# Linear attention in half steps between the units of the column projection, its values projected in token layout

## The reference, cut to what matters

```python
h = rmsnorm(x, norm_g)
proj = h @ w_in                       # split into g_q g_k g_v g_lr g_gate, f_*, m_*
log_a = log_sigmoid(g_lr @ w_alpha_up + b_alpha) / 16.0
# GLA: 4 heads, key width 48, value width 96, chunks of C = 64
b = cumsum(log_a, within a chunk)
q_dec = q * K ** -0.5 * exp(b); k_dec = k * exp(-b); k_to_end = k * exp(b_last - b)
attn = (q_dec @ k_dec.T) * causal
S_next = exp(b_last) * S + k_to_end.T @ v
o = attn @ v + q_dec @ S
o_gla = rmsnorm(o, gla_norm_g) * silu(g_gate)
# forgetting attention (6 heads, "fox") and attention over 256 memory tokens (4 heads, "att")
out = x + concat(o_gla, o_fox, o_mem) @ w_out   # then a final rmsnorm
```

## Time and profile before

| | before |
|---|---|
| runs, median | 1478.14 us |
| profiled execution, span | 1480.9 us |
| TensorE busy | 1312.8 us (89%) |
| VectorE, ScalarE, POOL busy | 665.6, 576.9, 411.6 us |
| mean granted clock of TensorE | 0.942 |
| column projection, matmuls L644 | x2112, 481.6 us busy |

### The profile page before, as it was taken

One profiled execution on the slowest core, in us unless ns is written; L12 is line 12 of the kernel. 1 busy time (PEld: TensorE's weight loads), 2 busy tenths in 40 slices (PEclk: granted clock), 3 DMA queues, 4 the chain that ended last, 5 costly groups with the idle time before them and its releaser, 6 DMA issues. The chain is left out here.

```text
span 1480.9 us, 20787 instructions
## 1 busy us (share of the span) xinstructions
PE 1312.8 (89%) x6576; PEld 1053.3 (71%) x6576; DVE 665.6 (45%) x1606; ACT 576.9 (39%) x1154; POOL 411.6 (28%) x408
## 2 busy tenths in 40 slices
PE   5898989999999999938785985999899999599997
PEld 4887878888888888814453663777678687478886
DVE  4563311110000011178874763888788798432222
ACT  3563201111111000047652874777677777421010
POOL 5223420111111011044553577222322422300000
PEclk9999999999999999959876987999999999799999
DMA  5453333331222121165321543422623520355553
GB/s 201 144 164 118 111 111 113 127 120 64 70 78 78 64 78 58 49 177 166 109 85 60 165 113 84 115 93 61 156 63 94 122 59 12 98 207 198 199 174 137
DMA packets 98908, 166.45 MB, mean 112 GB/s; under 512 B 10740, under 2 KB 51444, under 8 KB 96996
## 3 DMA queue, kind: packets, MB, share of 16 engines
q1 hardware_dynamic: 96088, 156.97, 34.7%
q10 hardware_dynamic: 2560, 8.39, 1.4%
q0 software_dynamic: 192, 0.33, 0.1%
HBM read 101.36 MB, written 64.29 MB: 112 GB/s over the span
## 5 line engine op out<-in xcount | busy, mean ns | idle before, releaser
L644 PE MATMUL col_cps<-h_T,tok_slot 128*128 128x512 f32 x2112 | 481.6, 390 | 4.0 <-POOL tok_slot L600 3.9
L644 PEld LDWEIGHTS col_cps<-h_T,tok_slot 128*128 128x128 f32 x2112 | 397.9, 188 | 87.8 <-issue 4.9
L1736 PE MATMUL out_yps<-out_w,out_mix 128*128 128x512 f32 x768 | 177.7, 394 | 19.3 <-DMA out_mix<-scr_mix 16.8
L1736 PEld LDWEIGHTS out_yps<-out_w,out_mix 128*128 128x128 f32 x768 | 145.7, 190 | 51.1 <-DMA out_mix<-scr_mix 17.1
L1540 ACT ACTIVATE fox_pT<-fox_tps 128x512 fp32r<-128x512 f32 x240 | 124.8, 531 | 88.2 <-PE fox_tps L1473 85.5
L1578 DVE TENSOR_SCALAR_CACHE_REDUCE fox_prob<-fox_sps 128x512 f32<-128x512 f32 (+2 forms) x240 | 142.0, 606 | 36.6 <-PE fox_sps L1463 33.7
L1589 DVE TENSOR_TENSOR fox_pT<-fox_tps,fox_pT 128x512 fp32r<-128x512 f32 x240 | 141.6, 604 | 21.7 <-ACT fox_pT L1540 20.9
L1473 PE MATMUL fox_tps<-all_ident,fox_prob 128*128 128x128 f32 x816 | 134.6, 278 | 15.1 <-ACT fox_prob L1532 8.2
L707 DVE COPY tok_xn<-col_cps 128x512 f32<-128x512 f32 x24 | 16.6, 692 | 287.4 <-PE col_cps L644 287.4
L1486 PE MATMUL fox_ops<-fox_pT,fox_v 128*128 128x512 f32 x480 | 137.2, 376 | 0.0
L1473 PEld LDWEIGHTS fox_tps<-all_ident,fox_prob 128*128 128x128 f32 x816 | 99.9, 141 | 45.1 <-ACT fox_prob L1532 11.6
(11 more groups left out here) (189 smaller groups left out, 1760.3 us busy)
## 6 DMA issues: line engine op xcount, KB each, us to landing
scr_split<-tok_w SPq DMA_DIRECT2D x64, 256.0 KB, 2.7
out_mix<-scr_mix SPq DMA_DIRECT2D x32, 512.0 KB, 4.2
tok_xin<-in_w_cols SPq DMA_DIRECT2D x22, 512.0 KB, 3.8
tok_xin<-in_x SPq DMA_DIRECT2D x16, 512.0 KB, 3.7
scr_gates<-tok_xn SPq DMA_DIRECT2D x32, 256.0 KB, 2.3
out_x<-in_x SPq DMA_DIRECT2D x16, 512.0 KB, 6.2
out<-out_o ACTq DMA_DIRECT2D x16, 512.0 KB, 4.9
scr_fox_v<-tok_vst SPq DMA_DIRECT2D x16, 384.0 KB, 2.9
```

The source lines that it names most:

```text
L644: mm = nc.tensor.matmul(cps[c][:, :], w[s][a_][:, kk, :], hT[b_][:, kk, c * CH:(c + 1) * CH], start=(kk == 0 and n == 0), stop=(kk == KT - ...
L1736: mm = nc.tensor.matmul(yps[s][:, c, :], mix[s][a][:, kk, :], w[b][:, kk, c * CH:(c + 1) * CH], start=(kk == 0 and n == 0), stop=(kk == MI ...
```

## The change

`project_columns` and `gated_linear_attention` become one stage, `columns_and_linear_attention`, written out over the 88 units instead of in loops. The tiles come in another order: 3 of GLA values, 3 of GLA queries and keys ("raw"), 3 of GLA gates, 8 split ones, 5 gates. TensorE has two banks for the units instead of four, since the linear attention takes the other six.

- A unit of the values is made in token layout: the normalised tokens are the stationary operand and the 128 weight columns move. That is 96 matmuls 128 wide in place of 24 that are 512 wide. The values' transposes (L920) and the copies of them on ScalarE are gone, and so is `vz`: the chunk states are made from 64 rows each, two for each pair of heads.
- Decay logits, Abs, Exp, Ln and the scan for 512 tokens lie ahead of units 6, 8, 10 and 12. Their `b` goes to scratch memory.
- Step n of the linear attention lies ahead of units 36 + 2n and 37 + 2n, one half at each. Inputs are loaded for one step (128 tokens) at a time; the Exps and the decayed queries and keys for step n + 1 are made in the second half of step n.
- The fills and first loads of the memory head and the fox head move to the start of the memory attention, on VectorE and SP ahead of all else.
- The tiles that the token stage leaves free lie elsewhere in SBUF, so that they can be released.

The diff's core:

```diff
+    KINDS = ["value"] * 3 + ["raw"] * 3 + ["gate"] * 3 + ["split"] * NSPLIT + ["gate"] * (NGATE - 3)
+    G0 = 36
+    def step_at(cls, u):
+        n, half = divmod(u - cls.G0, 2)
+        return (n, half) if -2 <= n <= cls.STEPS else (None, half)
...
+    Z_UNITS = {6 + 2 * g: g for g in range(NCH)}
...
+            @block.sync
...
+                for u in range(CU.UNITS):
+                    j, c = divmod(u, NCH)
+                    if c == 0 and j + 2 < NCOL:
+                        sp.wait_ge(w_lo, j + 1)
+                        sp.dma_start(w_raw[j % 2][:, :, :], w_cols[j + 2]).then_inc(cols_loaded[j % 2], 16)
+                    if u in Z_UNITS:
+                        g = Z_UNITS[u]
+                        if g == 0:
+                            sp.wait_ge(rows_stored, 80)
+                        if g >= 2:
+                            sp.wait_ge(z_done, PAIRS * (g - 1))
+                        sp.dma_start(lr[g % 2][:, :], scr.lr[:, g * CH:(g + 1) * CH]).then_inc(lr_loaded[g % 2], 16)
...
+                        if half_step == 0:
+                            if n + 2 < NS:
+                                load_inputs(n + 2)
+                            if 0 <= n < NS:
+                                load_gate(n)
+                        else:
+                            if 0 <= n + 1 < NS:
+                                load_values(n + 1)
+                            if n >= 1:
+                                store_mix(n - 1)
+                    store_unit(u)
...
+                def store_unit(u):
...
+                    sp.wait_ge(evacuated, u + 1)
...
+            @block.tensor
...
+                def decay_logits(g):
+                    pe.wait_ge(lr_loaded[g % 2], 16 * (g // 2 + 1))
...
+                for u in range(CU.UNITS):
+                    j, c = divmod(u, NCH)
+                    if u in Z_UNITS:
+                        decay_logits(Z_UNITS[u])
+                    n, half_step = CU.step_at(u)
+                    if n is not None:
+                        if half_step == 0:
+                            if n >= 1:
+                                outputs(n - 1)
+                            if 0 <= n < NS:
+                                key_side(n)
+                        else:
+                            if 0 <= n < NS:
+                                chunk_states(n)
+                            if n >= 1:
+                                transposed_outputs(n - 1)
+                    if c == 0:
+                        pe.wait_ge(w_lo, j + 1)
+                    if u >= 2:
+                        pe.wait_ge(evacuated, u - 1)
+                    if CU.KINDS[j] == "value":
+                        for i in range(CH // P):
+                            tokens = slice((4 * c + i) * P, (4 * c + i + 1) * P)
+                            for kk in range(KT):
+                                for r, (a_, b_) in enumerate(PASSES):
+                                    mm = nc.tensor.matmul(cps[u % 2][:, i * P:(i + 1) * P], hT[a_][:, kk, tokens],
+                                                          w[j % 2][b_][:, kk, :],
+                                                          start=(kk == 0 and r == 0), stop=(kk == KT - 1 and r == 2))
...
+                def key_side(n):
+                    if n:
+                        pe.wait_ge(k_copied, n)
+                    pe.wait_ge(prep_done, n + 1)
...
+                def chunk_states(n):
...
+                        for e in range(2):
+                            rows = slice(GLA_C * e, GLA_C * (e + 1))
+                            mm = nc.tensor.matmul(kvps[e][0:KR, p * W2:(p + 1) * W2], kt[rows, p * KR:(p + 1) * KR],
+                                                  vt[n % 2][rows, p * W2:(p + 1) * W2], start=True, stop=True)
...
+            @block.vector
...
+                        if half_step == 0:
+                            if 0 <= n < NS:
+                                mask(n)
+                            if n >= 1:
+                                normalise(n - 1)
+                            if 0 <= n + 1 < NS:
+                                decay_to_end(n + 1)
+                        else:
+                            if 0 <= n < NS:
+                                advance_states(n)
+                            if n >= 1:
+                                gated(n - 1)
+                            if 0 <= n + 1 < NS:
+                                decayed_queries(n + 1)
+                    evacuate(u)
...
+            @block.gpsimd
...
+                    if c == 0 and j >= 1 and j + 1 < NCOL:
+                        split(j + 1)
...
+                        if half_step == 0:
+                            if n >= 1:
+                                rstds(n - 1)
+                            if 0 <= n < NS:
+                                gates(n)
+                        else:
+                            if n >= 1:
+                                split_mix(n - 1)
+                            if 0 <= n + 1 < NS:
+                                decayed_keys(n + 1)
...
-def softmax_attention(nc, scr, ident, ident_b, mask, first, next_stages):
+def softmax_attention(nc, scr, ident, ident_b, mask, first, opening, next_stages):
...
+                for head in opening:
+                    head.first_loads(sp)
                 load_gate(0, 0)
                 load_gate(0, 1)
...
+                for head in opening:
+                    head.first_fill(nc.vector)
                 round_(0, False, prologue=True)
...
-            gated_linear_attention(nc, scr, ident, gla_mask, w_alpha_up, b_alpha, gla_norm_g, (att_head, fox_head))
-            softmax_attention(nc, scr, ident, ident_b, fox_mask, att_head, (weights_out,))
-        softmax_attention(nc, scr, ident, ident_b, fox_mask, fox_head, ())
+            softmax_attention(nc, scr, ident, ident_b, fox_mask, att_head, (att_head, fox_head), (weights_out,))
+        softmax_attention(nc, scr, ident, ident_b, fox_mask, fox_head, (), ())
```

More of the change, by code:

```diff
@@ L712, in gated_linear_attention, with gate_index, sends, sent_before @@
-def gated_linear_attention(nc, scr, ident, gla_mask, w_alpha_up, b_alpha, gla_norm_g, next_stages):
-    NG, GT = T // CH, CH
-    NS = T // P
-    ST = CH // P
+class ColumnUnits:
+    KINDS = ["value"] * 3 + ["raw"] * 3 + ["gate"] * 3 + ["split"] * NSPLIT + ["gate"] * (NGATE - 3)
+    FIRST = {"value": 0, "raw": 3, "split": 9}
+    UNITS = NCOL * NCH
+    G0 = 36
+    STEPS = T // P
+    @classmethod
+    def gate_index(cls, j):
+        return j - 6 if j < 9 else j - 9 - NSPLIT + 3
+    @classmethod
+    def sends(cls, u):
+        return 2 if cls.KINDS[u // NCH] == "split" else 1
+    @classmethod
+    def sent_before(cls, u):
+        return 16 * sum(cls.sends(i) for i in range(u % 2, u, 2))
+    @classmethod
+    def step_at(cls, u):
+        n, half = divmod(u - cls.G0, 2)
+        return (n, half) if -2 <= n <= cls.STEPS else (None, half)
@@ L743, in gated_linear_attention @@
         gn = k.sb("gn", [P, 3])
+        bf = k.sb("bf", [FOX_H, 1])
+        dec = [k.sb(f"dec{s}", [KR, PAIRS, P // GLA_C]) for s in range(2)]
+        ss, ms, rstd, half = (k.sb(n, [P, GLA_H]) for n in ("ss", "ms", "rstd", "half"))
+        cps = [k.ps(f"cps{s}", [P, CH]) for s in range(2)]
+        rows_ctx = ExitStack()
+        with rows_ctx:
+            kr = Pools(nc, rows_ctx, "rows")
+            rT, a_full = kr.sb("rT", [FGLR, T]), kr.sb("a", [FOX_H, T])
+            parts = [kr.sb(f"part{i}", [FOX_H, T], F32R) for i in (HI, LO)]
+            rps = kr.ps("rps", [P, T])
@@ new lines, in columns_and_linear_attention @@
+        f, a = rT[0:FOX_H, :], a_full[:, :]
+        decay_ctx = ExitStack()
+        with decay_ctx:
+            kz = Pools(nc, decay_ctx, "decay")
+            lr = [kz.sb(f"lr{s}", [GLA_R, CH]) for s in range(2)]
+            keep, zabs, la, bz = (kz.sb(n, [KR, PAIRS, CH]) for n in ("keep", "zabs", "la", "b"))
+        q, kk_, b = ([k.sb(f"{n}{s}", [KR, PAIRS, P]) for s in range(2)] for n in ("q", "k", "b"))
+        tail, ep, em, ee, kd, kte = (k.sb(n, [KR, PAIRS, P]) for n in "tail ep em ee kd kte".split())
@@ L772, in gated_linear_attention @@
[L772 to L785 removed]
+        kps, aps, ops, ots = (k.ps(n, [P, CH]) for n in ("kps", "aps", "ops", "ots"))
@@ new lines, in load_values, with load_gate @@
+                def load_values(n):
+                    if n >= 2:
+                        sp.wait_ge(o_done, n - 1)
+                    sp.dma_start(vt[n % 2][:, :], scr.gla_v[n]).then_inc(v_loaded[n % 2], 16)
+                def load_gate(n):
+                    if n >= 2:
+                        sp.wait_ge(mixed, n - 1)
+                    else:
+                        for parity in range(2):
+                            sp.wait_ge(stored[parity], CU.sent_before(4 * 9 + parity))
+                    sp.dma_start(gate[n % 2][:, :, :], scr.gates[0:3, :, n * P:(n + 1) * P].rearrange("j p t -> p j t")
```

(5 more changed lines are left out.)

990 lines of the change are left out of this document (408 added, 582 removed).

## The result

The changed kernel takes 1550.5 us, the kernel before 1478.1; the ratio is **1.0483, 95% interval 1.0461 to 1.0505**: slower by 4.8%. Forecast was 1486 (+8), the range ended at 1522. The direction was right, the size was not: some 60 us are missing from the sum, most of them because the narrow value matmuls ran at half the clock for much of their time.

The account below looks back on a forecast made before the run. TensorE fills the column projection; a chain through four engines bounds the linear attention. -179.7 + 16.6 + 70.7 + 76.3 + 8.8 + 16 + 4.4 - 5.0 = +8.1 on 1480.9, less 2.8: forecast 1486 us, range 1459 to 1522.

Parts of the forecast that it names:

- The value term, +70.7: Value units on TensorE: 1152 narrow matmuls at 0.118 us, 135.9 us, replace 65.2 us of wide ones; bounds +30 to +74.
- The rival of the falling clock: Value units: narrow matmuls leave the array half empty and the clock falls, up to +136 us, 1622; chance 0.03.
- The dips, +4.4: Clock dips after the four waits before the decay logits, 1.1 us lost in each.
- Decay logits, +8.8: Decay logits on TensorE between column units: eight matmuls, each two records of 1.11 us together.
- Waits for the rows, +16: TensorE waits for the low-rank rows `lr` before each of four decay-logit groups, 4.0 us each.
- Steps, +76.3: Linear attention's TensorE work between column units: 16 steps of 4.77 us, nothing taken for overlap or breaks.
- Opening of the memory attention, +16.6: Start of memory attention: loads ahead of the gates on SP delay POOL's first gate to 30.5 us from 13.9.
- the term's upper bound: Memory attention's opening: +24 us if the second head's loads are late too, by their own issue of 7.4.
- POOL's chain in the second half: Linear attention step, second half: 7.9 us chain against 9.1 before TensorE asks, margin 1.2, so costed at nothing.
- the third rival: POOL's chain late in the second half of each step: 2 us beyond the margin give 1518; chance 0.14.
- The standstill of 3.88 us: Column projection: TensorE's wait for the third tile's weight split on POOL disappears with its clock dip, -5.0 us.
- The stage removed, -179.7: The 183.3 us between column projection and memory attention go, except a stage change that remains.

Follow-up runs that it names:

- gates_first: Changed kernel with SP issuing both gates and the second head ahead of the fox head's first loads: 1545.3 and 1548.6 us, and 1606.3 and 1607.2.
- before_narrow: Kernel before with only its last three column tiles, the value tiles, as 1152 matmuls of 128 columns: 1542.8 us, ratio 1.042.
- spread_loads: Changed kernel with wide, transposed values, earlier low-rank rows and reordered loads (1445.6 us), now with the fox head's loads spread in pieces, output weights later: 1436.5 us.
- after_again: Changed kernel, unchanged, profiled a second time: 1604.9 and 1613.0 us.
- lr_early_warm: Changed kernel with low-rank rows loaded one unit earlier and 48 wide matmuls ahead of the first value unit: 1537.6 us, ratio 1.038.
- warm_again: lr_early_warm with 24 more wide matmuls in front of each of units 6, 8 and 10: 1495.7 us, ratio 1.010.
- halves_256: Changed kernel with value units as 576 matmuls of 256 columns, weights stationary, output not the reference's: 1449.8 us, ratio 0.980.

## Why the prediction was wrong

For the kernel after in its shorter executions the span is 1546.9 to 1548.8 where my sum had 1489.0: 58 to 60 us to account for. (The timed runs are 63 above the forecast, since the profiled execution of the kernel before was some 4 us longer than its median run.) Point by point, with `gates_first` for the value units:

- **The value term, +70.7, is the step that failed.** It measured 188.9 - 65.2 = 123.7 us, 53.0 more (and 181.6 in the long executions). The spacing was a good reading: 0.112 at the raised clock, for 0.118, which gives back 6.8. What failed was the clock: I took a pair's spacing from a place with 1.00 and multiplied it by 1152, as though the clock came with it. Half of the matmuls, the 576 behind the first wait, took 41.2 us for each 192 in place of 21.5, 59 more; the last 0.8 is the entry. The rival of the falling clock named the right quantity with a chance of 0.03, but not the cause that the runs show: the narrow matmuls did not bring the clock down (`before_narrow`); they only did not bring it back once a wait or the logits had. Its reason, "nothing in the trace runs like this for 136 us", was a reason for a wide range and not for a small chance.
- **The dips, +4.4, were read from the wrong neighbours.** In the earlier trace rows the clock came back within 4 us; there wide matmuls followed. Behind three of the four logit groups stand narrow ones, and there it did not come back at all. The term and the failed one are the same event: one break in the stream decides over hundreds of matmuls. Behind the fourth group, under wide matmuls, the clock takes 5.7 us to come back in `gates_first` (361.3 to 367.0), some 2.8 us lost for my 1.1.
- Decay logits, +8.8: 14.3 us, since most run at 0.50 (5.5 more). Waits for the rows, +16: 17.6.
- Steps, +76.3 with nothing for overlap and breaks: 4.12 in place of 4.77 a step, 10.4 less; the chunk states are 0.84 for my 1.30, which an overlap of matmuls on different rows could explain, as I had left open, and the scores 0.69 for 0.85. Breaks of 0.32 and 0.24 a step, 9.0 more. Together -1.4; taking nothing was right.
- Opening of the memory attention, +16.6: the stage is 125.6 for 104.2, +21.4. The first gate came at 31.6 after the start for my 30.5. The 5 us more seem to be the second head: TensorE waits 14 us for its loads, the case of the term's upper bound, which I had named and not taken; no run took this alone. That the block of issues is a cause was right (cutting it up won back 10 of the 21, `spread_loads`); that its place behind the gates would be harmless was not (`gates_first`), and was not part of the forecast.
- POOL's chain in the second half: no idle time of TensorE in any step; the third rival did not occur. The standstill of 3.88 us is gone, -5.0 as said. The stage removed, -179.7, stands: everything behind the memory attention is as long as before within 2 us (562.5 for 564.7).

Sum of the differences: 53.0 + 4.8 (opening) + 5.5 (logits) + 1.6 (waits) - 1.4 (steps) - 3.3 (three dips, now inside the first) = 60.2, against the 58 to 60 found. The stretches say the same without the points: from the first projection matmul to the memory attention's start `gates_first` takes 714.6 us (140.76 to 855.4) and the kernel before 668.8 (143.21 to 811.96), +45.9 for a forecast of -8.5; with the opening's 4.8 that is 59.2.

Open is why the clock stays at 0.50 from the start of the value units in some executions and not in others. In both profiles the clock fell in the wait at the change of stage (5.8 and 5.4 us). In the long one it never rose; in `gates_first` it rose about 1 us into the narrow units, which begin at 140.76, and that is the only rise that a trace here shows under them (the 16 transposes in front of them, from 137.23, may have their part in it). The first stretch is of the kernel after, the other two of `gates_first`:

```profile
136.00:138.00 2.00, 0.00 (x0) 0.80 0.40 120
```

```profile
140.00:142.00 2.00, 2.00 (x11) 0.56 0.00 0
142.00:144.00 2.00, 2.00 (x20) 1.00 0.04 8
```

The time between the kinds is that of the 576 matmuls up to the first decay logits at one level or the other: 123.1 us in `after_again`, 65.2 in `gates_first`, 57.9 apart.

## What to carry to other kernels

A spacing or a duration of TensorE is a number at one granted clock: before it is multiplied, ask which clock its row had, what raises the clock in the new place, and what stands there that may drop it (waits, but matmuls on few rows too). When a layout change narrows the moving side, compare it with staying wide and turning the result: here 48 transposes put 0.36 us between two units, some 4 us in all (and TensorE once stands 11 us for VectorE, which the slower narrow units had hidden), and the narrow form costs 63 at the best, 124 to 182 in fact. And when a block of issues on a queue makes a load late, moving that load ahead of the block may only make the next one late, as it did here; cutting the block into pieces won back half.

## What was not expected of the hardware

- The granted clock stayed at 0.50 through 280 us in which TensorE was busy for all but the waits, with matmuls 0.21 us apart (`PEclk` and stretches of the kernel after), the first 123 us of it without any gap (`after_again`); a raised one stayed at 1.00 through 129 us of the same matmuls (`before_narrow`).
- Four matmuls that contract over 16 rows, 1.97 us in all and with no gap on either side, were followed 2 us later by a fall to 0.50 (`lr_early_warm`). With wide matmuls behind them the clock fell at three groups of four and was back 3.4 us later (`warm_again`); under narrow ones it did not come back. Under 256 wide ones no stretch looked at stayed at 0.50 (`halves_256`).
- The chunk states as four matmuls of 64 rows and 192 columns (eight records) take 0.84 us of TensorE, where two of 128 rows and 384 columns took 1.30: matmuls on different halves of the rows seem to overlap; no run took this alone.
- The value matmuls at 128 columns start 0.112 apart at the raised clock, the 256 wide ones of the earlier trace rows 0.121, the 512 wide ones 0.226: from 256 down to 128 columns the narrower moving side saves next to nothing. Both forms load 128 columns of weights for each matmul; whether that load sets the pace no run took alone.
